# A float32 decoder trunk on one core: the preparation of its seven-product chunks in another order, and the low parts of gate slots by ScalarE's negation and a DMA that adds

## The chip, the cores and the metric

The kernel runs on one core of a Trainium2 chip. The metric is device time in microseconds. Engines are named as in the profile: PE (TensorE), DVE (VectorE), ACT (ScalarE), POOL (GpSimd) and SP (SyncE, which here issues the loads of weights). POOL also issues DMAs that add into their destination.

## What is computed

Two layers on 512 tokens of width 1024, float32. Each layer is a gated feed-forward stage, a mixing stage (sparse attention, pooling, memory attention) and a second feed-forward stage. The change lies in the four feed-forward stages:

```python
def rms_norm(x, g):
    xf = x.astype(jnp.float32)
    y = xf * lax.rsqrt(jnp.mean(xf * xf, axis=-1, keepdims=True) + EPS)
    return (y * g.astype(jnp.float32)).astype(x.dtype)

def swiglu(h, w_gate, w_up, w_down):
    return (jax.nn.silu(h @ w_gate) * (h @ w_up)) @ w_down
...
x = x + 0.5 * swiglu(rms_norm(x, ffn1_norm[l]), ffn1_gate[l], ffn1_up[l], ffn1_down[l])
```

The gate and up matrices are 1024 x 2816, the down matrix 2816 x 1024.

## The kernel before

**Arithmetic.** A float32 product is made of three PE passes on two rounded parts (`fp32r`): hi x hi, hi x lo, lo x hi (`passes`). So every operand needs a high part (ACT's rounding copy) and a low part. The low part comes in one of two ways: a subtraction value minus high on DVE or POOL; or ACT writes the rounded negative of the value into the low buffer and POOL issues a DMA that adds the value to it (`round_ahead` and `rest`).

**Tiles.** Activations are kept transposed, width on the 128 partitions, the 512 tokens along the free axis (`T`). A weight slot is 128 x 1024. SP loads slots into a ring of four in `raw`; `w_hi` and `w_lo` are rings of the same four places. 2816 is 22 chunks of 128 (`FC`); a chunk has a gate slot, an up slot and a down slot.

**A feed-forward stage.** PE first computes gate and up of 4 *classic* chunks (`CLASSIC`), slots 0 to 7, 24 matmuls of 512 columns each (`project_first`, `gate_up`). DVE takes a classic chunk out of PSUM, times the reciprocal root `r` (`evacuate`), ACT applies the silu (`classic_silu`), DVE multiplies (`gated_up`), ACT and DVE split the result for the down product (`classic_hi`, `classic_lo`). The other 18 chunks (`FAST`) are *seven-product* chunks: gate and up together are a 2 x 2 block product with seven multiplications instead of eight, halves of the width against halves of the tokens (`HALF` = 256). Each product is four 128-blocks times three passes, 12 matmuls of 256 columns.

- The token operands are `b11`, `b21`, `b22` (blocks of the normalized input `hn`, strided: four pieces of 256 columns) and `t1` to `t4` (sums of blocks, `token_sum`), all 128 x 1024, made once a stage: `op_round` on ACT for the high part, `op_rest` on DVE (`b11`, `b22`) or `rest_op` on POOL (`t1`, `b21`, `t2`, `t3`, `t4`) for the low.
- The weight operands are made for each chunk: four sums `s1` to `s4` of 128 x 512 (`weight_sum` on DVE, `sum_hi` on ACT, `rest_sum` on POOL), the gate slot itself (`gate_hi` on ACT, `gate_rest` on DVE) and the up slot's second half (`a22_hi`, `a22_rest`).
- The results are put together by `base_copy`, `silu0`, `silu1` on ACT and `up1_begin`, `up1_end`, `up0_end`, `gate1_begin`, `gate1_end`, `z_end` on DVE, half a tile each.

**Order.** Each engine runs a list written out by hand; nothing is planned at run time. PE's for period s is P1(s), P6(s), P4(s-1), P3(s-1), P2(s), P5(s), P7(s). Operands: P1 `b11`, P6 `t2`, P4 `t4`, P3 `b22`, P2 `b21`, P5 `t1`, P7 `t3`. P1 and P2 use the gate slot, P6, P5, P7 and P3 the sums 2, 1, 3 and 4. P4(0) needs `up1_begin(0)`, which needs P7(0); P2(0) needs `base_copy(0)`, which needs P1(0). Periods 0 and 1 are written out ahead of the loop, 16 follow, the last two apart on ACT and DVE. During the classic products and periods 0 and 1 the other engines make all the operands: this preparation is what the change orders anew. Then come the down products, 22 slots of 24 matmuls.

**Waits.** An engine runs its list in order, so an instruction that waits holds up all behind it. SP's refill of a gate slot waits for `s_sum_ready[4]`, DVE's last read of it. `root` makes the root of the mean square on ACT; the table for it is loaded when it gets there; DVE's reciprocal follows, and all of the preparation needs it.

Page lines: L684 is every matmul, L1643 and L1646 `evacuate`, L1653 `gated_up`, L1659 `classic_lo`, L1250 `classic_hi`, L1666 `normalize`, L1685 `token_sum`, L1691 `op_rest`, L613 `rest_op`, L1259 `op_round`, L1297 `gate_hi`, L1700 `gate_rest`, L1729 `weight_sum`, L1281 `sum_hi`, L621 `rest_sum`, L1319 `base_copy`, L1739 `up1_begin`, L1220 `root`, L549 `rest`, L1230 and L1231 `round_ahead`.

Of the kernel before, what the change touches and what calls it, by code (L numbers as in the profile page):

```python
# [128 lines left out]
def build(nc, x_t, mem_t, weights, pool_w, params, consts, out):  # L129
# [349 lines left out]
    with nc.Block() as block:  # L479

        @block.sync
        def _(sp):
# [57 lines left out]
        def _(pool):  # L540
# [66 lines left out]
            def ffn(l, e):  # L607
                base, q = FFN_BASE[e], l * 2 + e

                def rest_op(name):  # L610
# [14 lines left out]
                for n in range(BEGUN, 2 * CLASSIC):  # L625
                    rest(l, base + n)
                rest_op("t1")
                rest_op("b21")
                rest_op("t2")
                rest_sum(2, 0)  # L630
                rest_sum(1, 0)
                rest_sum(4, 0)
                rest_sum(3, 0)
                rest_op("t3")
                rest_sum(2, 1)
                rest_op("t4")
                rest_sum(1, 1)
                with pool.Fori(1, FAST - 1) as s:
# [1567 lines left out]
```

## Time and profile before

| | before |
|---|---|
| median of 3 runs | 1931.46 us (1931.42 to 1933.45) |
| profiled execution, time | 1928.9 us |
| its span | 1926.8 us |
| its mean granted clock of PE | 0.993 |
| PE busy | 1860.9 us, 97% |
| DVE busy | 1206.1 us, 63% |
| ACT busy | 1006.4 us, 52% |
| POOL busy | 744.9 us, 39% |
| `w_lo<-raw` DMAs issued by POOL | 179, of 512 KB |

Busy shares are means over stages with different limits. Where time can be won or lost is read from the stretches in which PE isn't busy, and from who was waited for there. A granted clock of 1.00 is 2.4 GHz and one of 0.50 is 1.2 GHz.

### The profile page before, as it was taken

To read this page: it belongs to the slowest core of one execution; us is meant where nothing else is said; L and a number is where in the kernel's file an instruction comes from. 1 tells how busy PE (TensorE), PEld (TensorE's weight loads), DVE (VectorE), ACT (ScalarE), POOL (GpSimd) and SP (SyncE) were. 2 spreads that over 40 slices of the span, in tenths; PEclk is the share of its full clock that TensorE was granted. 3 is DMA by queue.
4 is the path that set the end of the run, shared out by engine and by line. 5 is a ranking of instruction groups with operands and counts; after the bars stand their busy time and mean duration, and the time that the engine had idled before them with its cause. 6 is when DMAs were issued, how large, how long until landed. Compare 5 with 4: busy or idle time off the path is not lost.

```text
span 1926.8 us, 33602 instructions
## 1 busy us (share of the span) xinstructions
PE 1860.9 (97%) x11692; PEld 1633.7 (85%) x11692; DVE 1206.1 (63%) x1885; ACT 1006.4 (52%) x1610; POOL 744.9 (39%) x561
## 2 busy tenths in 40 slices
PE   7799999999999899999997999999999998999999
PEld 5799988877768699998887999888877787999887
DVE  6998821368753989841089988114786459988311
ACT  6444454575665544554464444546657564445542
POOL 2566621112511656641126666111216016666310
PEclk9899999999999999999999999999999999999999
DMA  7233388888237423368862333888781373333785
GB/s 213 79 106 103 100 202 193 184 198 193 72 88 175 120 88 109 106 161 195 193 163 77 101 100 117 206 195 196 183 203 39 86 183 110 99 109 105 181 196 140
DMA packets 75391, 272.92 MB, mean 142 GB/s; under 512 B 8496, under 2 KB 8752, under 8 KB 75056
## 3 DMA queue, kind: packets, MB, share of 16 engines
q1 hardware_dynamic: 48960, 175.67, 28.4%
q0 software_dynamic: 25776, 93.86, 27.1%
q10 hardware_dynamic: 576, 2.36, 0.3%
q8 instruction: 47, 0.77, 0.2%
q14 instruction: 32, 0.26, 0.0%
HBM read 175.91 MB, written 2.10 MB: 92 GB/s over the span
## 4 chain that ended last, share of the span: by engine, by line
PE 84%; DVE 9%; issue 3%; ACT 1%; DMA 1%; DVEq 0%; SPq 0%; ACTq 0%; POOLq 0%
PE bank L684 83%; DVE s_sum L1729 2%; PE bank L1122 1%; DVE hn L1666 1%; DMA w_lo<-raw 1%; DVE w_lo L1700 1%; DVE t L1653 1%; DVE a_hi L1659 1%; DVE t_sum L1685 1%; DVE b_lo L1691 0%; DVE h_lo L1601 0%; DVE t L1646 0%; DMA raw<-weights 0%; DVE zf L1777 0%; DVE t L1643 0%
## 5 line engine op out<-in xcount | busy, mean ns | idle before, releaser
L549 POOL DMA_DIRECT2D w_lo<-raw x179 | 154.6, 873 | 803.2 <-ACT w_lo L1231 758.1
L621 POOL TENSOR_TENSOR w_lo<-s_sum,w_hi 128x512 fp32r<-128x512 f32 x216 | 338.8, 1582 | 285.9 <-ACT w_hi L1281 285.7
L684 PE MATMUL bank<-t_hi,w_hi 128*128 128x256 f32 x1152 | 330.7, 287 | 38.3 <-DVE zf L1739 27.4
L1230 ACT ACTIVATE w_hi<-raw 128x1024 fp32r<-128x1024 f32 x163 | 172.3, 1057 | 344.3 <-PE bank L684 325.6
L684 PE MATMUL bank<-t_lo,w_hi 128*128 128x256 f32 x1152 | 328.8, 285 | 0.0
L684 PE MATMUL bank<-t_hi,w_lo 128*128 128x256 f32 x1152 | 328.7, 285 | 0.0
L684 PE MATMUL bank<-a_hi,w_hi 128*128 (+1 forms) x832 | 324.8, 390 | 0.0
L684 PE MATMUL bank<-a_lo,w_hi 128*128 (+1 forms) x832 | 323.8, 389 | 0.0
L684 PE MATMUL bank<-a_lo,w_lo 128*128 (+1 forms) x704 | 273.9, 389 | 0.0
L1281 ACT ACTIVATE w_hi<-s_sum 128x512 fp32r<-128x512 f32 x216 | 132.3, 624 | 245.4 <-DVE s_sum L1729 234.6
L684 PEld LDWEIGHTS bank<-t_hi,w_hi 128*128 128x128 f32 x1152 | 223.7, 194 | 41.8 <-issue 39.7
L1863 DVE TENSOR_TENSOR a_hi<-zf,a_lo x72 | 49.8, 692 | 327.1 <-ACT a_lo L1402 327.1
L684 PEld LDWEIGHTS bank<-t_hi,w_lo 128*128 128x128 f32 x1152 | 224.1, 194 | 0.0
L684 PEld LDWEIGHTS bank<-t_lo,w_hi 128*128 128x128 f32 x1152 | 224.0, 194 | 0.0
L684 PE MATMUL bank<-h_hi,w_hi 128*128 128x512 f32 x496 | 199.6, 402 | 13.7 <-ACT h_hi L1208 8.0
L684 PE MATMUL bank<-h_hi,w_lo 128*128 128x512 f32 x496 | 194.6, 392 | 0.0
L684 PEld LDWEIGHTS bank<-a_hi,w_hi 128*128 128x128 f32 x832 | 156.2, 188 | 33.8 <-issue 1.4
L684 PEld LDWEIGHTS bank<-a_lo,w_hi 128*128 128x128 f32 x832 | 156.2, 188 | 32.1
L684 PE MATMUL bank<-h_lo,w_hi 128*128 128x512 f32 x496 | 179.0, 390 | 0.1
L1231 ACT ACTIVATE w_lo<-raw 128x1024 fp32r<-128x1024 f32 x163 | 169.9, 1043 | 0.0
L684 PE MATMUL bank<-b_hi,w_hi 128*128 128x256 f32 x576 | 164.0, 285 | 5.0 <-ACT base_p L1319 5.0
L684 PE MATMUL bank<-b_lo,w_hi 128*128 128x256 f32 x576 | 163.6, 284 | 0.0
(206 smaller groups left out, 3958.9 us busy)
## 6 DMA issues: line engine op xcount, KB each, us to landing
raw<-weights SPq DMA_DIRECT2D x326, 512.0 KB, 3.8
w_lo<-raw POOLq DMA_DIRECT2D x179, 512.0 KB, 5.9
x<-x_t SPq DMA_DIRECT2D x4, 512.0 KB, 7.4
mem<-mem_t ACTq DMA_DIRECT2D x2, 1024.0 KB, 7.6
out_t<-x SPq DMA_DIRECT2D x8, 256.0 KB, 2.1
const<-consts SPq DMA_DIRECT2D x1, 481.5 KB, 10.5
wpool<-pool_w ACTq DMA_DIRECT2D x2, 128.0 KB, 7.5
par<-params SPq DMA_DIRECT2D x1, 38.0 KB, 3.4
```

The source lines that it names most:

```text
L549: G.dma_start(w_lo[:, s], raw[:, s], accum_op=ALU.add).then_inc(w_ready[pos], 16)
L621: G.tensor_tensor(out=fast_weight(l, e, product, 0, True), in0=s_sum[i - 1][:, :], in1=fast_weight(l, e, product, 0, False).bitcast(f32), ...
L684: return nc.tensor.matmul(out_, lhsT, rhs, start=start, stop=stop, skip_group_check=True)
L1122: last = nc.tensor.transpose(bank[2 + n % 2][:, b * P:(b + 1) * P], prob[n % 4][:, b * P:(b + 1) * P], con(C_ID, P))
L1230: nc.scalar.activation(w_hi[:, s], raw[:, s], ACT.Copy).then_inc(w_hi_done, 1)
L1231: nc.scalar.activation(w_lo[:, s], raw[:, s], ACT.Copy, scale=-1.0)\
L1281: nc.scalar.activation(fast_weight(l, e, product, 0, False), s_sum[i - 1][:, :], ACT.Copy).then_inc(s_hi_ready[i], 1)
L1653: V.tensor_tensor(out=chunk(t2, f % 2), in0=chunk(t1, f % 2), in1=chunk(t2, f % 2), op=ALU.mult).then_inc(prod_ready, 1)
L1659: V.tensor_tensor(out=chunk(a_hi, f), in0=chunk(t2, f % 2), in1=chunk(a_lo, f).bitcast(f32), op=ALU.subtract).then_inc(a_lo_ready, 1)
L1666: last = V.scalar_tensor_tensor(out=chunk(hn, k), in0=chunk(x, k), scalar=par[:, ds(l * PARAMS + (gain + k), 1)], in1=r[:, :], op0=ALU.mul ...
L1729: V.tensor_tensor(out=s_sum[i - 1][:, :], in0=a, in1=b, op=op).then_inc(s_sum_ready[i], 1)
L1863: V.tensor_tensor(out=a_hi[:, ds(f * T, T)], in0=zf[:, ds(f * T, T)], in1=a_lo[:, ds(f * T, T)].bitcast(f32), op=ALU.subtract).then_inc(a_ ...
```

## The change

- **Low parts of gate slots.** `gate_hi` also writes the negative of the slot into `w_lo`, and POOL's new `rest_gate` issues the adding DMA; DVE's `gate_rest` is gone. PE waits for the DMA, with one semaphore for even and one for odd chunks. SP's refill of a gate slot waits for it too.
- **Token operands.** `t1` and `b22` get their low part by `op_negate` (ACT) and a DMA (`rest_op`, POOL); `b21`, `t2`, `t3`, `t4` by `op_rest` on DVE. The order of `op_round`s differs, and the places of `op_hi` and `op_lo` start at `a_lo`'s beginning.
- **Low parts of sums.** Of chunk 0, and of `s2` of chunk 1, on DVE (`sum_rest`); the later ones on POOL as before.
- **Classic chunks.** `evacuate` is cut into `gate_out` and `up_out`, which stand apart. `gated_up` writes to `zf`, and the split for the down product moves to the stage's end (`split_hi`, `split_lo`). `classic_hi` and `classic_lo` are gone.
- **Root.** Its table is loaded ahead of the wait for the sums; `round_ahead(base)` stands ahead of `root` in all four stages, `round_ahead(base + 1)` ahead of the first `classic_silu`.

Cut to its core:

```diff
-        _at = (a_lo_at + (CLASSIC + 4 * _j) * tile_b) if _j < 4 else (h_at + 4 * (_j - 4) * tile_b)
+        _at = (a_lo_at + 4 * _j * tile_b) if _j < 5 else (h_at + 4 * (_j - 5) * tile_b)
...
+                    if not up:
+                        sp.wait_ge(g_lo_ready[s % 2], 16 * i + gate_lo_count(l * 2 + e, s, s % 2))
...
                 def rest_op(name):
-                    pool.wait_ge(op_hi_ready[name], q + 1)
-                    G.tensor_tensor(out=wide(op_lo[name]), in0=op_source[name],
-                                    in1=wide(op_hi[name]).bitcast(f32),
-                                    op=ALU.subtract).then_inc(op_lo_ready[name], 1)
+                    wait_apart(pool, op_neg_ready, q * len(DMA_RESTS) + DMA_RESTS.index(name) + 1)
+                    G.dma_start(wide(op_lo[name]), op_source[name], accum_op=ALU.add)\
+                        .then_inc(op_lo_ready[name], 16)
...
+                def rest_gate(s, par):
+                    wait_apart(pool, g_neg_ready, s + (q * FAST + 1))
+                    to = fast_slot(l, e, par)
+                    p = place_of(l, base + 2 * (CLASSIC + par)) * SLOT
+                    G.dma_start(w_lo[:, to:to + SLOT], raw[:, p:p + SLOT], accum_op=ALU.add)\
+                        .then_inc(g_lo_ready[par], 16)
...
-                    pe.wait_ge(g_lo_ready, at(s))
+                    pe.wait_ge(g_lo_ready[par], gate_lo_count(q, s, par))
...
             def root(l, ph):
+                nc.scalar.preload_act_table(ACT.Sqrt)
...
+                def op_negate(name):
+                    nc.scalar.activation(wide(op_lo[name]), op_source[name], ACT.Copy, scale=-1.0)\
+                        .then_inc(op_neg_ready, 1)
...
                     nc.scalar.activation(w_hi[:, to:to + SLOT], raw[:, p:p + SLOT],
                                          ACT.Copy).then_inc(g_hi_ready, 1)
+                    nc.scalar.activation(w_lo[:, to:to + SLOT], raw[:, p:p + SLOT],
+                                         ACT.Copy, scale=-1.0).then_inc(g_neg_ready, 1)
...
+                def split_hi(f):
+                    if isinstance(f, int) and f < CLASSIC:
+                        act.wait_ge(prod_ready, (q + 1) * CLASSIC)
+                        act.wait_ge(prod_done[1], at(FAST - 1))
+                    else:
+                        act.wait_ge(zf_ready, f + (q * FAST + 1 - CLASSIC))
+                    nc.scalar.activation(a_lo[:, ds(f * T, T)], zf[:, ds(f * T, T)], ACT.Copy)\
+                        .then_inc(a_hi_ready, 1)
...
+                    else:
+                        split_hi(0)
                     a22_hi(s, par)
+                    if isinstance(s, int) and s + 1 >= FAST:
+                        split_hi(1)
                     sum_hi(4, s)
...
                 silu0(FAST - 1, 1)
+                silu1(FAST - 1, 1)
+                split_hi(2)
                 round_down(3)
-                silu1(FAST - 1, 1)
+                split_hi(3)
...
+                def gate_out(f):
+                    if f >= 2:
+                        dve.wait_ge(prod_ready, q * CLASSIC + f - 1)
+                    dve.wait_ge(slot_done, l * SLOTS + base + 2 * f + (RING + 1))
...
-                    V.tensor_tensor(out=chunk(t2, f % 2), in0=chunk(t1, f % 2), in1=chunk(t2, f % 2),
+                    V.tensor_tensor(out=chunk(zf, f), in0=chunk(t1, f % 2), in1=chunk(t2, f % 2),
                                     op=ALU.mult).then_inc(prod_ready, 1)
...
                     if more:
-                        gate_rest(s + 1, 1 - par)
                         weight_sum(1, s + 1, 1 - par)
```

What this does to the lists is shown where the prediction needs it. Names there are the program's, with a buffer number behind; `base_p` is what `base_copy` writes, `s_sum1` to `s_sum4` are the sums, `bank4` and `bank0` are PSUM banks. ACT at the beginning of the seven-product chunks of the first stage, before:

```order
L1281 ACTIVATE w_hi_53<-s_sum3_69 128x512
L1259 ACTIVATE t3_hi_109<-t3_sum_99 128x1024
L1319 ACTIVATE base_p_117<-bank4 128x256
L1288 ACTIVATE w_hi_53<-raw_52 128x512
L1259 ACTIVATE b22_hi_113<-hn_96 128x1024
L1281 ACTIVATE w_hi_53<-s_sum2_68 128x512
L1259 ACTIVATE t4_hi_111<-t4_sum_100 128x1024
```

and now:

```order
L1301 ACTIVATE w_hi_53<-s_sum3_69 128x512
L1308 ACTIVATE w_hi_53<-raw_52 128x512
L1341 ACTIVATE base_p_117<-bank4 128x256
L1274 ACTIVATE t4_hi_111<-t4_sum_100 128x1024
L1301 ACTIVATE w_hi_53<-s_sum2_68 128x512
L1274 ACTIVATE b22_hi_113<-hn_96 128x1024
L1279 ACTIVATE b22_lo_114<-hn_96 128x1024
```

`t3`'s rounding and a classic `a_lo` are no longer ahead of the first `base_p`; the up slot's half is, and `b22` has two instructions, behind `t4` and `s_sum2`.

DVE at the same place, up to the first `zf` from a bank (`up1_begin(0)`), before:

```order
L1759 TENSOR_TENSOR part_u_118<-bank5,base_p_117 128x256
L1729 TENSOR_TENSOR s_sum2_68<-raw_52,s_sum1_67 128x512
L1707 TENSOR_TENSOR w_lo_54<-raw_52,w_hi_53 128x512
L1729 TENSOR_TENSOR s_sum3_69<-raw_52 128x512
L1691 TENSOR_TENSOR b22_lo_114<-hn_96,b22_hi_113 128x1024
L1729 TENSOR_TENSOR s_sum4_70<-raw_52,s_sum2_68 128x512
L1643 TENSOR_TENSOR t1_58<-bank2,r_57 128x512
L1646 TENSOR_TENSOR t2_59<-bank3,r_57 128x512
L1653 TENSOR_TENSOR t2_59<-t1_58,t2_59 128x512
L1659 TENSOR_TENSOR a_hi_55<-t2_59,a_lo_56 128x512
L1739 TENSOR_TENSOR zf_95<-bank5,base_p_117 128x256
```

and now:

```order
L1789 TENSOR_TENSOR part_u_118<-bank5,base_p_117 128x256
L1758 TENSOR_TENSOR s4_lo_116<-s_sum4_70,s4_hi_115 128x512
L1729 TENSOR_TENSOR w_lo_54<-raw_52,w_hi_53 128x512
L1758 TENSOR_TENSOR w_lo_54<-s_sum2_68,w_hi_53 128x512
L1722 TENSOR_TENSOR t4_lo_112<-t4_sum_100,t4_hi_111 128x1024
L1751 TENSOR_TENSOR s_sum3_69<-raw_52 128x512
L1677 TENSOR_TENSOR t2_59<-bank3,r_57 128x512
L1684 TENSOR_TENSOR zf_95<-t1_58,t2_59 128x512
L1751 TENSOR_TENSOR s_sum4_70<-raw_52,s_sum2_68 128x512
L1769 TENSOR_TENSOR zf_95<-bank5,base_p_117 128x256
```

The rests of `s_sum4` and `s_sum2` and of `t4` stand where sums and `b22`'s rest stood, and no `a_hi` is made here.

POOL from the last classic slots on, before:

```order
L549 DMA w_lo_54<-raw_52 128x1024 x5
L613 TENSOR_TENSOR t1_lo_108<-t1_sum_97,t1_hi_107 128x1024
L613 TENSOR_TENSOR b21_lo_106<-hn_96,b21_hi_105 128x1024
L613 TENSOR_TENSOR t2_lo_104<-t2_sum_98,t2_hi_103 128x1024
L621 TENSOR_TENSOR w_lo_54<-s_sum2_68,w_hi_53 128x512
L621 TENSOR_TENSOR w_lo_54<-s_sum1_67,w_hi_53 128x512
L621 TENSOR_TENSOR s4_lo_116<-s_sum4_70,s4_hi_115 128x512
L621 TENSOR_TENSOR w_lo_54<-s_sum3_69,w_hi_53 128x512
```

and now:

```order
L558 DMA w_lo_54<-raw_52 128x1024 x4
L622 DMA t1_lo_108<-t1_sum_97 128x1024
L558 DMA w_lo_54<-raw_52 128x1024
L638 DMA w_lo_54<-raw_52 128x1024 x2
L622 DMA b22_lo_114<-hn_96 128x4x256
L638 DMA w_lo_54<-raw_52 128x1024
L629 TENSOR_TENSOR w_lo_54<-s_sum1_67,w_hi_53 128x512
```

The seven subtractions of the first piece are gone from POOL; the second piece has DMAs for `t1`, gate slots 0 and 1, `b22` and gate slot 2.

## Rows read from the trace of the kernel before

**Rows 1.** Stretches, PE: start:end, us, busy (x instructions), PEclk, DMA share, GB/s.

```profile
59.36:94.21 34.85, 24.82 (x169) 0.85 0.20 62
654.09:687.97 33.88, 23.40 (x169) 0.90 0.21 63
1014.32:1047.89 33.57, 22.50 (x170) 0.95 0.18 63
1608.40:1641.58 33.18, 23.86 (x170) 0.90 0.22 64
94.21:252.85 158.64, 158.63 (x1320) 1.00 0.36 110
```

**Rows 2.** Timeline of PE: start, us, instruction, count, [idle before <-releaser].

```profile
35.87 0.50 PE L684 MATMUL bank<-h_hi,w_hi 128*128 128x512 f32 x1 [1.46 <-DVE t L1646]
42.90 0.50 PE L684 MATMUL bank<-h_hi,w_hi 128*128 128x512 f32 x1 [1.26 <-DMA w_lo<-raw]
...
658.56 0.39 PE L684 MATMUL bank<-b_hi,w_hi 128*128 128x256 f32 x1 [1.25 <-ACT base_p L1319]
664.10 0.35 PE L684 MATMUL bank<-t_hi,w_hi 128*128 128x256 f32 x1 [2.40 <-POOL t_lo L613]
674.34 0.55 PE L684 MATMUL bank<-t_hi,w_hi 128*128 128x256 f32 x1 [5.70 <-DVE zf L1739]
...
687.97 0.35 PE L684 MATMUL bank<-t_hi,w_hi 128*128 128x256 f32 x1 [1.14 <-DVE zf L1739]
```

**Rows 3.** Stretch after the longest wait, columns as in Rows 1.

```profile
674.30:679.30 5.00, 4.96 (x23) 0.50 0.02 3
```

**Rows 4.** Timeline of DVE in the second feed-forward stage.

```profile
623.66 3.35 DVE L1615 RECIPROCAL r<-r 128x512 f32<-128x512 f32 x1 [3.62 <-ACT r L1220]
627.16 0.69 DVE L1643 TENSOR_TENSOR t<-bank,r 128x512 f32<-128x512 f32 x1
628.37 2.73 DVE L1666 SCALAR_TENSOR_TENSOR hn<-x,par,r 128x512 f32<-128x512 f32 x4
...
642.07 3.43 DVE L1700 TENSOR_TENSOR w_lo<-raw,w_hi 128x1024 fp32r<-128x1024 f32 x1
645.42 2.89 DVE L1659 TENSOR_TENSOR a_hi<-t,a_lo 128x512 fp32r<-128x512 f32 x1
...
673.82 0.41 DVE L1739 TENSOR_TENSOR zf<-bank,base_p 128x256 f32<-128x256 f32 x1
...
688.27 1.21 DVE L1700 TENSOR_TENSOR w_lo<-raw,w_hi 128x1024 fp32r<-128x1024 f32 x1
689.40 0.68 DVE L1729 TENSOR_TENSOR s_sum<-raw 128x512 f32<-128x512 f32 x1
690.00 0.42 DVE L1759 TENSOR_TENSOR part_u<-bank,base_p 128x256 f32<-128x256 f32 x1
```

**Rows 5.** Timeline of POOL, beside the two long rows of Rows 4.

```profile
641.47 2.95 POOL L613 TENSOR_TENSOR b_lo<-hn,b_hi 128x1024 fp32r<-128x1024 f32 x1 [1.72 <-ACT b_hi L1259]
```

**Rows 6.** Timeline of ACT in the second feed-forward stage.

```profile
621.65 1.28 ACT L1220 ACT_TABLE_LOAD   x1 [4.80 <-PE bank L684]
622.94 0.69 ACT L1220 ACTIVATE r<-bank,const 128x512 f32<-128x512 f32 x1
...
630.32 1.04 ACT L1230 ACTIVATE w_hi<-raw 128x1024 fp32r<-128x1024 f32 x1
631.27 1.04 ACT L1231 ACTIVATE w_lo<-raw 128x1024 fp32r<-128x1024 f32 x1
```

**Rows 7.** Tile w_lo, POOL: landings in 600:700, in 410:600 and in 94:252.

```profile
DMA to landing us min/median/max: 4.5/6.2/8.6
...
DMA to landing us min/median/max: 4.6/6.6/11.5
...
DMA to landing us min/median/max: 4.6/4.6/4.6
```

**Rows 8.** Timeline in the loop of the second stage, ACT and PE.

```profile
774.27 1.04 ACT L1297 ACTIVATE w_hi<-raw 128x1024 fp32r<-128x1024 f32 x1
...
785.96 0.28 PE L684 MATMUL bank<-b_hi,w_hi 128*128 128x256 f32 x1
```

**Rows 9.** Timeline at the loop's end: fourth down slot's rounding, first down product.

```profile
848.96 1.06 ACT L1330 ACTIVATE w_hi<-raw 128x1024 fp32r<-128x1024 f32 x1 [0.98 <-PE bank L684]
...
850.14 0.40 PE L684 MATMUL bank<-a_lo,w_hi 128*128 128x512 f32 x1
```

More of the change, by code:

```diff
@@ L623, in rest_sum, with period @@
                                     op=ALU.subtract).then_inc(s_lo_ready[i], 1)
[L625 to L638, printed above, removed]
+                def rest_gate(s, par):
[4 more added lines that the diff above has]
+                        .then_inc(g_lo_ready[par], 16)
+                def period(s, par):
                     rest_sum(3, s)
@@ L641, in ffn @@
                     rest_sum(4, s)
+                    if not (isinstance(s, int) and s + 2 >= FAST):
+                        rest_gate(s + 2, par)
                     rest_sum(1, s + 1)
+                for n in range(BEGUN, 2 * CLASSIC - 1):
+                    rest(l, base + n)
+                rest_op("t1")
+                rest(l, base + 2 * CLASSIC - 1)
+                rest_gate(0, 0)
+                rest_gate(1, 1)
+                rest_op("b22")
+                rest_gate(2, 0)
+                rest_sum(1, 1)
+                period(1, 1)
+                with pool.Fori(1, FAST // 2 - 1) as i:
+                    period(i * 2, 0)
+                    period(i * 2 + 1, 1)
+                period(FAST - 2, 0)
                 rest_sum(3, FAST - 1)
@@ L1236, in ffn @@
                 prepare(l, 2 * e, (G_FFN1, G_FFN2)[e], base - 1)
-                ahead = l == 0 and e == 0
-                if ahead:
-                    round_ahead(l, base)
+                round_ahead(l, base)
                 root(l, 2 * e)
@@ L1778, in z_end @@
                                     op=ALU.mult).then_inc(zf_ready, 1)
[L1780 removed]
+                gate_out(0)
+                up_out(0)
                 normalize(0)
[L1782 removed]
+                gate_out(1)
                 token_sum("t1")
+                up_out(1)
+                normalize(1)
                 op_rest("b11")
[L1785 removed]
                 token_sum("t2")
                 gated_up(0)
[L1788 to L1789 removed]
+                op_rest("t2")
+                op_rest("b21")
+                token_sum("t3")
+                gate_out(2)
+                up_out(2)
                 weight_sum(1, 0, 0)
                 weight_sum(2, 0, 0)
[L1792 removed]
                 token_sum("t4")
[L1794 removed]
+                gated_up(1)
+                op_rest("t3")
                 weight_sum(3, 0, 0)
                 weight_sum(4, 0, 0)
[L1797 to L1799 removed]
+                sum_rest(2, 0)
+                sum_rest(1, 0)
+                gated_up(2)
+                gate_out(3)
+                sum_rest(3, 0)
                 weight_sum(1, 1, 1)
+                weight_sum(2, 1, 1)
                 gate1_begin(0, 0)
[L1803 removed]
+                sum_rest(4, 0)
                 a22_rest(0, 0)
+                sum_rest(2, 1)
+                op_rest("t4")
                 weight_sum(3, 1, 1)
[L1806 removed]
+                up_out(3)
+                gated_up(3)
                 weight_sum(4, 1, 1)
[L1808 to L1810 removed]
                 def period(s, par):
@@ L1838, in tail @@
                     z_end(s, par)
-                up1_begin(0, 0)
-                up1_end(0, 0)
-                gate_rest(2, 0)
-                weight_sum(1, 2, 0)
-                gate1_begin(1, 1)
-                weight_sum(2, 2, 0)
-                up0_end(0, 0)
-                weight_sum(3, 2, 0)
-                a22_rest(1, 1)
-                gate1_end(0, 0)
-                gated_up(3)
-                classic_lo(3)
-                z_end(0, 0)
-                weight_sum(4, 2, 0)
+                period(1, 1)
                 with dve.Fori(1, FAST // 2 - 1) as i:
```

97 lines of the change are left out of this document (36 added, 61 removed).

## The prediction

> **What bounds the kernel now.** I read the busy time by stretches first, since the question is where TensorE (PE) isn't full. In the loop of a feed-forward stage it is: from 94.21 it runs 1320 matmuls in 158.64 us, busy all the time at full clock [rows 1]. A product has 12 matmuls, so that is 110 products at 158.64 / 110 = 1.442 us, and a period of seven takes 10.1 us. What the change gives VectorE (DVE) there is worth nothing, unless it makes PE wait.
>
> The four stretches above it are the openings: from a stage's first product P1(0) to P4(1), the fourteenth product after it (Pn(s) is product n of chunk s). They hold 14 products, 20.19 us at the loop's pace, and take 34.85, 33.88, 33.57 and 33.18 us [rows 1]. So 14.66, 13.69, 13.38 and 12.99 us are lost, 54.7 in all. PE's timeline shows where, in the second stage: 1.25 us until ScalarE (ACT) copied `base_p`; 2.40 until POOL had `t3`'s low part; 5.70 and 1.14 until DVE wrote `zf` (`up1_begin`) [rows 2]. That is 10.5 us; the rest is the clock, which after the 5.70 us wait stands at 0.50, the lower of its levels, with 23 matmuls in 5 us [rows 3], where the loop's pace makes 42. In stage one, ahead of its opening, 1.46 us go to DVE's first emptying of banks and 1.26 to a classic slot's low part [rows 2]: 2.7 us. **What there is to gain is 54.7 + 2.7 = 57.4 us.**
>
> Why DVE is late: a 1024-wide difference takes 1.21 us when it is alone, with the next start 1.13 later, and a 512-wide sum 0.60; but 3.43 and 2.89 us (512 wide!) beside a POOL subtraction of 2.95 us [rows 4, 5]. The Trainium skill (SBUF — State Buffer, the list under its door diagram) says that a DVE instruction with two SBUF inputs and a GpSimd one that reads SBUF hold a port pair exclusively, for the whole instruction; the trace agrees: 2.89 us for one of 0.68.
>
> **The change, part by part**, in the second stage's times; t0 = 654.09 is P1(0).
>
> *DVE's queue until `up1_begin(0)`.* Before, DVE goes from 627.16 to 673.82 [rows 4], 46.7 us. Its instructions alone: 8 emptyings, 8 weight sums, 3 `gated_up`, 3 `classic_lo` and `a22_rest`, 23 at 0.60 = 13.8; 8 at 1.13 (4 token sums, 2 `op_rest`, 2 `gate_rest`) = 9.0; `normalize`, twice 2.7 [rows 4]; `gate1_begin` 0.35: 28.6 us. Most of the other 18 us is waiting beside POOL's 11 subtractions. The change takes off 2 `gate_rest`, 3 `classic_lo` and `b22`'s rest, -(2.26 + 1.8 + 1.13) = -5.2; it adds the rests of `t2`, `b21`, `t3`, `t4` and five `sum_rest`, 4.5 + 3.0 = +7.5; `gated_up(3)` comes forward, +0.6. Sum 31.5, and no POOL arithmetic stands beside it before `rest_sum(1,1)`. Starting at 627, DVE could be done at 658.6, and `up1_begin(0)` can't start before P7(0) ends at t0 + 5 x 1.442 + 0.2 = 661.5. PE wants it at P4(0), t0 + 7 x 1.442 = 664.18. Walked instruction by instruction behind what each waits for, `t4`'s rest ends at 660.5, then `weight_sum(3)`, `up_out(3)`, `gated_up(3)` and `weight_sum(4)` take 2.4, and `up1_begin` ends at 663.4: 0.8 us ahead. The waits of 5.70 and 1.14 and the slow clock go. What is late next is `b22`, below.
>
> *`t3` on DVE.* Its rest ends near 649.6, wanted at P7(0), 659.9: the 2.40 us go.
>
> *`base_copy(0)`.* ACT had `t3` in front of it; now it has `sum_hi(3,0)` and `a22_hi`, done near 655.5, when P1(0) ends (655.7). The copy is ready at 656.1 and P2(0) wants it at 657.0: the 1.25 us go. In stage one they don't: classic work starts later there, DVE reaches `gate_out(3)` 2.5 us after P1(0) starts, ACT waits for it in `classic_silu(3)`, and 0.5 + 0.5 + 0.5 + 0.3 us later comes the copy, at t0 + 4.6 where P2 wants it at t0 + 2.9. I leave **1.75 us** of wait there.
>
> *`b22` by negation and DMA, the new dependence.* ACT: P6(0) ends at 657.2; `sum_hi(2,1)` half of a 1024-wide one, 0.5, then `b22`'s rounding and negation at 0.95 each (630.32 to 631.27) [rows 6]: 659.7. POOL has only this to do, so the DMA is issued at once. P3(0) wants it at t0 + 8 x 1.442 = 665.6: it may take 5.9 us. Accumulations of the same 512 KB took 4.5 to 8.6 us around this stage, 6.2 in the middle [rows 7]. No row has one with a source in four pieces of 1 KB per partition; below nothing it can't cost, since it still has a start, a copy and an end. Bounds 4.5 and 11.5 (the longest of any stage) [rows 7]; I take 7.2, the middle row and one more for the pieces. **Wait 1.3 us** per stage, 2.1 in stage one, where ACT's lateness narrows the room to 5.1.
>
> By the Trainium skill (DMA: Bandwidth & Descriptors, the SWDGE fit) such a DMA takes about 2.0 us + bytes / 436 GB/s, 3.2 us here, and (same page, why small descriptors are slow) copies inside SBUF don't pay for short pieces. The rows' smallest, 4.5, already lies above the fit, so I don't use it; by it `b22` would cost no wait (rival 1).
>
> *`t1` and the gate slots of chunks 0 and 1.* `t1` is negated near 634 and `gate 0` near 640, both wanted after 654; gate 1 near 648.5, wanted at 661.3. Each has over 12 us for a DMA. POOL's queue puts `t1` ahead of the last classic slot's rest, 0.95 us of ACT later than before; that slot is wanted 3 us or more after it lands. Nothing.
>
> *`root`.* The table load of 1.28 us comes ahead of the wait for the sums [rows 6]. In stage one that starts DVE 1.28 earlier and takes nearly all of the 1.46 away; `round_ahead(base + 1)` now stands ahead of the first `silu`, about 3 us earlier, and takes the 1.26. In the others `round_ahead(base)`, 1.9 us, goes in front, into the 4.80 us in which ACT idled [rows 6]; 0.8 us of the load's gain are left, which no one waits for. In `mix` nobody waits for it either.
>
> *The loop.* DVE loses `gate_rest` (1.13 or more), ACT gains 0.95, POOL an issue. New is a chain: ACT's gate rounding starts at 774.27, with the negation it ends at 776.2, and the P1 that reads this slot starts at 785.96 [rows 8], so the DMA has 9.8 us; the one accumulation inside a loop took 4.6 [rows 7]. No wait. SP's refill of the slot now waits for that landing too, but the sums that it waits for anyway come at the end of DVE's period, about when P1 starts, later than this landing.
>
> *The end.* `split_hi(2)` and `silu1` go ahead of the fourth down slot's rounding, which moves from 848.96 to about 851.7 [rows 9]: in memory by 862 even at 8.6 us. Down products begin at 850.14 [rows 9] and 24 matmuls take some 5.4 us a slot, so it is wanted at 866. `split_hi(0)` and `(1)` go where ACT waited for products. Nothing.
>
> **Sum.** Stage one: 14.66 + 2.7 - 0.1 - 1.75 - 2.1 = 13.4. The others: 13.69 + 13.38 + 12.99 - 3 x 1.3 = 36.2. Gain 49.6. The profiled execution took 1928.9 us (span 1926.8), 2.6 under the median 1931.5: 1931.5 - 49.6 = **1881.9 us**.
>
> **Rivals.**
> 1. *No new wait*: `b22` lands in under 5.9 us and ACT keeps up. For it: the quickest landings, 4.5 and 4.6 us, leave over a microsecond [rows 7]. Gain 57.4 - 1.75 - 0.1 = 55.5: 1876. The fit of the Trainium skill's page DMA: Bandwidth & Descriptors would give this too.
> 2. *`b22` late*: it lands in 11.5 us. Waits 3 x 5.6 + 6.4 = 23.2; and waits of 5.7 us brought the low clock for 5 us, half of which is lost: 4 x 2.5 = 10. Gain 55.5 - 33.2 = 22.3: 1909. For it: four times as many pieces; against it: DMA share about 0.2 in the openings [rows 1].
> 3. *ACT becomes the bound of the openings*: it has three gate negations, two operand negations more by `P4(1)`, 4.8 us, and its queue stands still at every wait. If each opening keeps 3 us more of waiting, some with low clock: gain 38, 1894.
> 4. *Slower*: the loop's chain. From P2(s) to P1(s+2) the slot passes through ACT, POOL and the DMA in two periods. If landings there exceed 9.8 us, every second period waits for the excess; 4 stages x 8 pairs = 32 of them. From 9.8 + 49.6 / 32 = 11.35 us on the change is slower; with the 11.5 of rows 7 it loses 54 and ends at 1936, and each further us costs 32. For it: loads run there at a DMA share of 0.36, and an accumulation's own share comes on top. Against it: 4.6 us measured at that share.
> 5. *It doesn't do what it says*: the openings are bound by something the walk misses, and half of the gain comes: 1906.
>
> **How the numbers follow.** Forecast 0.55, rival one 0.15, two 0.08, three 0.12, four 0.04, five 0.06. Leaving out the slow end of two and five, and four, the range is 1874 to 1903. About 0.2% (3.9 us) is what a measurement of this kernel can tell from no change. Faster 0.94, same 0.02, slower 0.04.
>
> **What would show it.** Right: the openings (P1(0) to P4(1)) take 22 to 24 us, with no `zf` wait and full clock; one wait on a DMA of `b_lo` remains at P3(0); the loop still runs 1320 matmuls in 158.6 us; DVE idles before `up1_begin(0)`; 512-wide DVE instructions of the opening take 0.7 us. Wrong: loop products wait for the DMA of `w_lo`; PE waits for ACT's `base_p` or `w_hi` in every stage; landings of the strided copy above 9 us.

## The result, and the profile after

The changed kernel takes 1918.57 us (median of 4 runs, 1917.35 to 1918.94), the kernel before, measured again beside it, 1932.26 (1931.42 to 1933.45): a ratio of 0.9928, 95% interval 0.991 to 0.9945. It is faster by 13.7 us, where the prediction had 49.6, and above the range. The profiled execution took 1918.83 us, its span 1916.9.

The openings gave what was forecast in sum, and the loops didn't stay as they were. First the stretches, as in [rows 1] (start:end, us, busy of PE, PEld, DVE, ACT and POOL with their instructions, PEclk, DMA share, GB/s; PEld is PE's loading of weights). Two openings, each with the loop behind it, then the loops of stages three and four:

```profile
56.80:80.89 24.09, 22.11 (x169) 21.73 (x168) 18.95 (x30) 15.20 (x25) 9.51 (x8) 0.93 0.72 164
80.89:248.73 167.84, 161.44 (x1322) 159.02 (x1320) 117.59 (x172) 86.51 (x156) 100.97 (x78) 1.00 0.57 145
651.17:671.82 20.65, 20.38 (x169) 20.20 (x168) 16.29 (x25) 14.40 (x24) 9.34 (x8) 1.00 0.67 161
671.82:839.60 167.78, 161.17 (x1322) 158.92 (x1320) 117.33 (x172) 86.26 (x156) 101.17 (x78) 1.00 0.57 145
...
1030.50:1198.30 167.80, 161.15 (x1322) 158.91 (x1320) 117.56 (x172) 86.47 (x156) 100.40 (x77) 1.00 0.56 144
1622.10:1789.90 167.80, 161.31 (x1322) 158.98 (x1320) 117.53 (x172) 86.48 (x156) 100.99 (x78) 1.00 0.58 145
```

The openings of stages one and two fell from 34.85 and 33.88 us to 24.09 and 20.65, at a granted clock of 0.93 and 1.00; those of stages three and four went from 33.57 and 33.18 to 22.71 (1007.79 to 1030.50) and 20.75 (1601.35 to 1622.10). That is 47.3 us, and stage one's P1(0) starts at 56.80 instead of 59.36, 2.6 more. But each loop, 158.64 us before, takes 167.8: 9.2 us more in each of the four, 36.7 in all. 47.3 + 2.6 - 36.7 = 13.2.

PE's waits (what it waited for, us in total, times, longest) have one entry for the loops. Of its 29.3 us some 26 lie in them; the other part of the 36.7 stands in PE's busy time, 161.2 to 161.4 us a loop where it was 158.6:

```profile
PE bank L705 <- DVE zf L1769: 29.3, 51, 1.1
```

The waits of the openings, where [rows 2] had 1.25, 2.40, 5.70 and 1.14 us in one stage, are these four and a fifth, of 0.36 us, in stage four:

```profile
61.57 0.38 PE L705 MATMUL bank<-b_hi,w_hi 128*128 128x256 f32 x1 [1.73 <-ACT base_p L1341]
...
72.19 0.36 PE L705 MATMUL bank<-b_hi,s_hi 128*128 128x256 f32 x1 [0.24 <-DMA b_lo<-hn]
...
663.11 0.36 PE L705 MATMUL bank<-b_hi,s_hi 128*128 128x256 f32 x1 [0.27 <-DMA b_lo<-hn]
...
1020.34 0.35 PE L705 MATMUL bank<-t_hi,w_hi 128*128 128x256 f32 x1 [2.31 <-issue]
```

Why is the loop longer? Nothing in it waits for a landing; PE waits for DVE's `zf` (`up1_begin`) once a period. So I followed DVE back, through one period of stage one's loop. ACT, POOL and DVE (timelines: start, us, line, ..., idle before and its releaser):

```profile
120.01 1.05 ACT L1317 ACTIVATE w_hi<-raw 128x1024 fp32r<-128x1024 f32 x1
120.95 1.04 ACT L1319 ACTIVATE w_lo<-raw 128x1024 fp32r<-128x1024 f32 x1
121.90 1.14 ACT L1301 ACTIVATE w_hi<-s_sum 128x512 fp32r<-128x512 f32 x2
...
130.51 0.42 ACT L1334 ACTIVATE gated<-gated 128x256 f32<-128x256 f32 x1 [1.30 <-DVE gated L1796]
130.83 1.04 ACT L1317 ACTIVATE w_hi<-raw 128x1024 fp32r<-128x1024 f32 x1
...
122.57 0.87 POOL L638 DMA_DIRECT2D w_lo<-raw  x1 [2.10 <-ACT w_lo L1319]
123.18 2.83 POOL L629 TENSOR_TENSOR w_lo<-s_sum,w_hi 128x512 fp32r<-128x512 f32 x2
...
124.91 1.66 DVE L1751 TENSOR_TENSOR s_sum<-raw 128x512 f32<-128x512 f32 x1 [2.42 <-POOL w_lo L629]
126.49 0.41 DVE L1789 TENSOR_TENSOR part_u<-bank,base_p 128x256 f32<-128x256 f32 x1
...
128.72 1.42 DVE L1729 TENSOR_TENSOR w_lo<-raw,w_hi 128x512 fp32r<-128x512 f32 x1 [0.29 <-ACT w_hi L1308]
130.06 0.41 DVE L1796 TENSOR_TENSOR gated<-bank,part_u 128x256 f32<-128x256 f32 x1
```

Read as a ring: ACT rounds a gate slot (120.01) and negates it (120.95 to 121.99). POOL starts the DMA on it 0.58 us later, 122.57. Behind that in POOL's queue stands subtraction 1, 123.18, and DVE's sum 1 of the next chunk waits for it, since it overwrites the sum that the subtraction reads: DVE is idle for 2.42 us. Sum 1 starts at 124.91; behind it in DVE's queue are sums 2 and 3, `a22_rest` and `gate1_end`, ending near 130.5; ACT's `silu1` waits for `gate1_end`, and behind `silu1` stands the next gate rounding, 130.83. The ring is 10.82 us round; PE's work in it is 10.10.

Before, the first half was two instructions shorter. ACT went from the gate rounding at 774.27 straight to `sum_hi(1)`, and POOL straight to the subtraction:

```profile
775.22 0.61 ACT L1281 ACTIVATE w_hi<-s_sum 128x512 fp32r<-128x512 f32 x1
...
775.91 3.54 POOL L621 TENSOR_TENSOR w_lo<-s_sum,w_hi 128x512 fp32r<-128x512 f32 x2 [1.18 <-ACT w_hi L1281]
...
777.07 1.22 DVE L1700 TENSOR_TENSOR w_lo<-raw,w_hi 128x1024 fp32r<-128x1024 f32 x1
778.21 1.78 DVE L1729 TENSOR_TENSOR s_sum<-raw 128x512 f32<-128x512 f32 x1
```

From the gate rounding to the start of subtraction 1 it was 1.64 us, now 3.17; from there to sum 1 the way got shorter, so that the gate rounding to sum 1 took 3.94 us and takes 4.90. The instruction that the change takes off DVE, `gate_rest` at 777.07, stood in between: subtraction 1 was done at 777.21, and sum 1 came 1.0 us later, behind `gate_rest`.

### The profile page after: what moved, and what is told of

Same layout as the page of the kernel before. It is cut to its first block and busy times, and to the rows that moved or that the text cites. A ratio compares the mean times of both kernels' runs of the same rounds, so it can differ in the third digit from the quotient of the medians.

```text
span 1916.9 us, 33816 instructions
## 1 busy us (share of the span) xinstructions
PE 1863.9 (97%) x11692; PEld 1630.5 (85%) x11692; DVE 1074.6 (56%) x1845; ACT 1069.5 (56%) x1690; POOL 672.8 (35%) x601
## 5 line engine op out<-in xcount | busy, mean ns | idle before, releaser
L705 PE MATMUL bank<-t_hi,w_hi 128*128 128x256 f32 x1152 | 330.6, 287 | 31.9 <-DVE zf L1769 29.3
L629 POOL TENSOR_TENSOR w_lo<-s_sum,w_hi 128x512 fp32r<-128x512 f32 x200 | 277.8, 1494 | 153.1 <-ACT w_hi L1301 153.0
L1301 ACT ACTIVATE w_hi<-s_sum 128x512 fp32r<-128x512 f32 x216 | 127.3, 621 | 257.9 <-DVE s_sum L1751 256.9
L1690 DVE TENSOR_TENSOR a_hi<-zf,a_lo (+1 forms) x88 | 68.4, 781 | 321.9 <-ACT a_lo L1363 321.8
L1751 DVE TENSOR_TENSOR s_sum<-raw 128x512 f32<-128x512 f32 x144 | 160.4, 1114 | 146.4 <-POOL w_lo L629 146.4
```

The costliest lines, as they stand in the source:

```text
L629: G.tensor_tensor(out=fast_weight(l, e, product, 0, True), in0=s_sum[i - 1][:, :], in1=fast_weight(l, e, product, 0, False).bitcast(f32), ...
L705: return nc.tensor.matmul(out_, lhsT, rhs, start=start, stop=stop, skip_group_check=True)
L1301: nc.scalar.activation(fast_weight(l, e, product, 0, False), s_sum[i - 1][:, :], ACT.Copy).then_inc(s_hi_ready[i], 1)
L1690: V.tensor_tensor(out=a_hi[:, ds(f * T, T)], in0=zf[:, ds(f * T, T)], in1=a_lo[:, ds(f * T, T)].bitcast(f32), op=ALU.subtract).then_inc(a_ ...
L1751: V.tensor_tensor(out=s_sum[i - 1][:, :], in0=a, in1=b, op=op).then_inc(s_sum_ready[i], 1)
```

## The experiments

**Theory (ring).** The loop's period is the longer of PE's 10.10 us and this ring, and what was added to it is ACT's negation and POOL's DMA issue ahead of subtraction 1. **Rivals.** The negation alone sets it; the added traffic of the DMAs slows the engines or the loads; or the new order of the preparation does it, whatever is done with the gates.

**Both behind subtraction 1** (e1). ACT negates behind `sum_hi(1)`, POOL issues the DMA behind `rest_sum(1)`:

```diff
 # ACT
-                    gate_hi(s + 2, par)            # with the negation in it
+                    gate_hi(s + 2, par)
 ...                 sum_hi(1, s + 1)
+                    gate_neg(s + 2, par)
 # POOL, period
+                    rest_sum(1, s + 1)
                     if not (isinstance(s, int) and s + 2 >= FAST):
                         rest_gate(s + 2, par)
-                    rest_sum(1, s + 1)
```

> Edit to the changed kernel: in each period ACT's negation of the gate slot stands behind its rounding of sum 1, and POOL's adding DMA behind its subtraction for sum 1. Theory C (a ring of waits around the engines): in the changed kernel's loop each period takes 10.83 us, the length of a ring ACT gate rounding 0.95, negation 0.95, rounding of sum 1, POOL's DMA issue 0.61, its subtraction for sum 1, DVE's sum 1 of the next chunk and what follows on DVE, ACT's silu, gate rounding. Without the negation and the issue it is 9.27, under PE's 10.10, so the loop goes back to 10.10 a period and 158.6 us a stage instead of 167.8: 1918.6 - 37 = 1882 us. Rival D (the added DMA traffic slows the loop: DMA share 0.57 instead of 0.36): nothing moved but the order, 1915 to 1920. Rival O (the new openings hand the loop over in a worse phase): as D.

1881.87 us (1880.06 to 1883.72), ratio 0.9751 (0.9734 to 0.9767). The whole loss is gone, with the same DMAs and the same instructions. PE's waits for `zf` are 2.4 us in 4 times, one near each loop's end.

**One half each** (e2, e6). In e2 only POOL's half of that edit, ACT's as in the changed kernel; in e6 only ACT's half.

> Edit to the changed kernel: POOL's part alone, the adding DMA behind the subtraction for sum 1; ACT's list as in the changed kernel. Theory C: the ring shrinks by 0.61 us (DMA issue to the next start on POOL), to 10.22, 0.12 over PE's 10.10; of 37 us some 31 come back: about 1888 us. If ACT's negation alone made the loss, nothing: 1918. Rival D or O: 1915 to 1920.

> Edit to the changed kernel: ACT's part alone, the negation behind the rounding of sum 1; POOL still issues the DMA ahead of its subtraction for sum 1. Theory R: POOL's list is in order and the DMA now waits 0.52 us longer for the negation, so the ring grows to about 11.35 us a period: 14 periods x 4 x 0.52 = 29 more, 1948 us. If ACT's delay of the rounding of sum 1 were the cause by itself: 1882.

e2: 1914.69 us (1914.48 to 1915.14), ratio 0.9921 (0.9904 to 0.9937); I had expected 1888, and was wrong. By its time alone the rival that the negation by itself makes the loss would stand; e7 below takes it away. e6: 1950.34 us (two runs, 1949.47 and 1951.2), ratio 1.0098 (1.0078 to 1.0118), as expected: gate roundings at 110.68 and 122.04, so the period is 11.36. There the negation, one `sum_hi` later, still has subtraction 1 queued behind it through the DMA issue.

Why e2 gained nearly nothing stands in its timelines, POOL's, then DVE's:

```profile
120.60 1.29 POOL L629 TENSOR_TENSOR w_lo<-s_sum,w_hi 128x512 fp32r<-128x512 f32 x1 [2.12 <-ACT w_hi L1301]
121.83 0.87 POOL L638 DMA_DIRECT2D w_lo<-raw  x1
122.44 1.59 POOL L629 TENSOR_TENSOR w_lo<-s_sum,w_hi 128x512 fp32r<-128x512 f32 x1
...
122.03 2.56 DVE L1751 TENSOR_TENSOR s_sum<-raw 128x512 f32<-128x512 f32 x1 [1.53 <-POOL w_lo L629]
```

DVE's sum 1 is released earlier, but it begins 0.20 us after POOL's DMA issue, with subtraction 3 right behind the issue, and takes 2.56 us instead of the 1.66 of the changed kernel: it ends 0.56 us behind subtraction 3 (124.03). What was won ahead of sum 1 is lost in it.

In e1 POOL's order is the same, and sum 1 takes 2.56 us in some periods there too, and 0.68 in others. POOL, then DVE:

```profile
109.34 0.87 POOL L638 DMA_DIRECT2D w_lo<-raw  x1
...
119.49 0.87 POOL L638 DMA_DIRECT2D w_lo<-raw  x1
...
109.53 2.56 DVE L1761 TENSOR_TENSOR s_sum<-raw 128x512 f32<-128x512 f32 x1
...
119.63 0.68 DVE L1761 TENSOR_TENSOR s_sum<-raw 128x512 f32<-128x512 f32 x1
```

But without the negation ahead it starts 3.28 us after the gate rounding (106.25), where it is 4.02 in e2, and that leaves room for the long sum: the next gate rounding comes at 116.40, 10.15 us on, the one after it 10.01 us later.

**One more copy on ACT** (e3). In ACT's list, behind the gate's rounding and negation, one more 1024-wide copy, to a tile that no one reads:

```diff
+                        nc.scalar.activation(spare[:, :], raw[:, ...], ACT.Copy)
```

> Edit to the changed kernel: one more ACT copy of 128x1024 (0.95 us) into unused memory, between the gate rounding and the negation in each period. Theory C: every period becomes 10.83 + 0.95 = 11.78 us, and the periods wait from the loop's start: some 15 periods x 4 stages x 0.95 = 57 us more: 1975 us. Rival D or O, where ACT with 4 us of idle time a period is no link: no change, 1915 to 1922.

1923.49 us (1921.91 to 1927.72), ratio 0.9968 (0.9951 to 0.9986): 4.9 us above the changed kernel, not 56. The expectation speaks of a copy between rounding and negation, where it would delay the DMA; built was a copy behind both, which delays `sum_hi(1)` alone. So the run does not test the 57 us, but it says which leg of the ring is the long one:

```profile
121.84 1.04 ACT L1414 ACTIVATE spare<-raw 128x1024 fp32r<-128x1024 f32 x1
122.79 1.14 ACT L1302 ACTIVATE w_hi<-s_sum 128x512 fp32r<-128x512 f32 x2
...
122.51 0.87 POOL L639 DMA_DIRECT2D w_lo<-raw  x1 [2.10 <-ACT w_lo L1320]
123.50 2.54 POOL L630 TENSOR_TENSOR w_lo<-s_sum,w_hi 128x512 fp32r<-128x512 f32 x2
```

The copy delays `sum_hi(1)` by 0.9 us, but POOL spends most of that time on the DMA anyway (0.58 us to start it, 0.6 until the next instruction starts). Subtraction 1 starts 0.99 us after the issue instead of 0.61, and sum 1 1.42 us after that (124.92) instead of 1.73; the period is 10.91 instead of 10.82. ACT's way to subtraction 1 runs beside POOL's and had slack for most of the copy. The long leg is negation, start of the DMA, its issue.

**POOL's half, done otherwise** (e7). So the DMA must go out of the way of subtraction 1, and of sum 1 too: behind subtractions 1 and 3. ACT's list is that of the changed kernel.

```diff
 # POOL, period
                     rest_sum(3, s)
+                    if not (isinstance(s, int) and s == 1):
+                        rest_gate(s + 1, 1 - par)
                     rest_sum(2, s + 1)
                     rest_sum(4, s)
-                    if not (isinstance(s, int) and s + 2 >= FAST):
-                        rest_gate(s + 2, par)
                     rest_sum(1, s + 1)
```

> Edit to the changed kernel: POOL issues a gate slot's DMA behind both subtractions (sums 1 and 3); ACT's list as in the changed kernel, with the negation ahead of sum 1. Theory R: sum 1's subtraction starts when its rounding is done, 0.9 us sooner, nothing of POOL's DMA stands between it and DVE's next sum 1, as it did with the DMA between the two subtractions (there DVE's instruction took 2.56 us): ring 9.9 us, under PE's 10.10: 1882 us. If the negation's 0.95 us on ACT is enough for the loss: 1910 to 1918.

1882.08 us (1881.49 to 1882.51), ratio 0.9745 (0.9729 to 0.9762): as good as e1, with the negation where it was. POOL, then DVE:

```profile
118.91 2.55 POOL L629 TENSOR_TENSOR w_lo<-s_sum,w_hi 128x512 fp32r<-128x512 f32 x2 [2.12 <-ACT w_hi L1301]
121.40 0.86 POOL L638 DMA_DIRECT2D w_lo<-raw  x1
...
120.35 1.66 DVE L1751 TENSOR_TENSOR s_sum<-raw 128x512 f32<-128x512 f32 x1 [0.87 <-POOL w_lo L629]
```

The gate rounding stands at 116.32 in this trace, so it is 4.03 us to sum 1 instead of 4.90. By that I estimate the ring at 10.82 - 0.87 = 9.95 us, below PE's 10.10; the loop shows only PE's period, so its own length can't be read there. The place of one DMA issue in POOL's queue is worth 36.5 us.

**Smaller DMAs** (e4, one run). Order and count as in the changed kernel, but in the gate slots of the seven-product chunks the DMA covers 64 of the 1024 columns; the rest stays the negated value, so this computes something else.

```diff
-                    G.dma_start(w_lo[:, to:to + SLOT], raw[:, p:p + SLOT], accum_op=ALU.add)\
+                    G.dma_start(w_lo[:, to:to + 64], raw[:, p:p + 64], accum_op=ALU.add)\
```

> Edit to the changed kernel: the adding DMA of a gate slot covers 64 of its 1024 columns (the rest of the low part isn't made, so the output is not the reference's); same instructions, same waits. Theory R (ring through ACT's negation and POOL's DMA issue, 0.58 us to its start and 0.87 for it, ahead of the subtraction for sum 1): bytes are no link of it, period stays 10.8 us, time 1912 to 1920. Rival D (traffic of the added DMAs slows the loop): period 10.10, about 1882.

1917.91 us, against 1918.57: taking 15/16 of these DMAs' bytes away gives nothing back that one run could show, where the rival wanted 36 us. And e1 and e7 lose nothing with all of the bytes.

**The gates of the loop on DVE** (e5). The preparation of the changed kernel, its gates 0 and 1 by DMA, and from gate 2 on the kernel before's `gate_rest` on DVE:

```diff
 # ACT: gate_hi rounds only; gate_neg(0, 0) and gate_neg(1, 1) stand in the opening
 # POOL, period
-                    if not (isinstance(s, int) and s + 2 >= FAST):
-                        rest_gate(s + 2, par)
 # DVE, period
+                        gate_rest(s + 1, 1 - par)
```

> Edit to the changed kernel: its preparation stays, with gate slots 0 and 1 by negation and DMA, but from chunk 2 on DVE subtracts the gate slot's low part as in the kernel before. Theory C: no negation and no issue in the ring; the loop takes 158.6 us a stage and the openings keep what they gained: 1882 us. Rival O (the openings spoil the loop): loops stay over 160 us and the time stays above 1900.

1884.47 us (1881.75 to 1884.92), ratio 0.9761 (0.9745 to 0.9777). So the gain of the change is the preparation's, and the gate slots of the loop bring no more to it than the 2.4 us between this run and e7 (1882.08), whose ranges overlap. From the gate rounding to sum 1 it is 4.02 us here, with `gate_rest` in between, as in e7 without it.

**The gates alone** (e8). The kernel before with its own preparation, and all gate slots by negation and DMA, issued ahead of subtraction 1:

```diff
 # in the kernel before; ACT
+                    nc.scalar.activation(w_lo[:, to:to + SLOT], raw[:, p:p + SLOT],
+                                         ACT.Copy, scale=-1.0).then_inc(g_neg_ready, 1)
 # POOL, period
+                    if not (isinstance(s, int) and s + 2 >= FAST):
+                        rest_gate(s + 2, par)
                     rest_sum(1, s + 1)
 # DVE, period
-                        gate_rest(s + 1, 1 - par)
```

> The kernel before, with its own preparation, and the change's second half alone: the low part of every gate slot of the seven-product chunks by ScalarE's negation and GpSimd's accumulating DMA, issued ahead of subtraction 1 as in the changed kernel. The ring theory says that the loop's period becomes 10.8 us here too, whatever prepares it: 9.2 us more in each of four loops, 37 in all, while the openings shed at most a few us with three 1024-wide VectorE differences less: 1950 to 1968 us, 1958 the likeliest. The rival, that the new preparation leaves the loop in another phase and the gate slots alone would be harmless, says 1925 to 1932 us.

1966.06 us (1965.49 to 1967.68), ratio 1.0187 (1.0169 to 1.0204): 35.1 us slower than the kernel before. ACT's gate roundings at 779.24 and 790.08 and POOL's DMA issues at 770.96 and 781.80 give the period: 10.84. Four times 9.2 is 36.8, so about 2 us came back elsewhere, presumably in the openings; they weren't measured apart. The loss is the same without the new preparation.

**Better openings, two tries** (e9, e10). e9 is e1 with two edits in the opening: ACT's `classic_silu(3)`, which waits for DVE, behind `base_copy(0,0)`, and gate 2's negation and DMA behind `sum_hi(1,1)` and subtraction 1. e10 is e7 with the first of the two alone.

```diff
 # ACT, opening; both
-                classic_silu(3)
                 sum_hi(3, 0, 2 * CLASSIC - 1)
                 a22_hi(0, 0)
                 base_copy(0, 0)
+                classic_silu(3)
 # POOL, opening; e9
+                rest_sum(1, 1)
                 rest_gate(2, 0)
-                rest_sum(1, 1)
```

> The kernel with both late (1881.87 us) with two more edits: the last classic silu behind the first base_copy on ACT (takes the 1.7 us wait of the first opening), and gate slot 2's negation and DMA behind sum 1 as in the loop (may take the 2.3 us wait of the third opening). Expected 1878 to 1881 us.

> The version with GpSimd's DMA behind subtractions 1 and 3, and in the opening one edit of the combined version alone: classic_silu(3) behind base_copy(0,0). ScalarE's queue in stage one's opening then comes two microseconds earlier, and so does GpSimd's first subtraction. If the combined version lost its gain because GpSimd's work now stands beside VectorE's normalization and weight sum 4 (a wait of 3.56 us at P4(0) of stage one in place of 0.52), that wait comes here too, base_copy's 1.3 goes, and the time is 1882 to 1885 us. If it lost it by its other edit in the opening (the gate's DMA behind subtraction 1 there), the wait stays at 0.5 and the time is 1879 to 1881 us.

e9: 1884.28 us (1883.05 to 1885.09), ratio 0.9754 (0.9738 to 0.977), no better than e1. e10: 1876.47 us (1874.8 to 1877.23), ratio 0.9723 (0.9706 to 0.9739), the fastest here. Both lose `base_copy`'s wait in stage one (1.3 us in e1 and e7). In e9 a wait of 3.56 us at P4(0) of stage one takes its place; in e10 it is 1.19. DVE in e9, then in e10, the same two instructions (`zf<-t,t` of the emptying and weight sum 4):

```profile
65.79 1.82 DVE L1693 TENSOR_TENSOR zf<-t,t 128x512 f32<-128x512 f32 x1
67.54 2.23 DVE L1760 TENSOR_TENSOR s_sum<-raw,s_sum 128x512 f32<-128x512 f32 x1
```

```profile
64.78 0.69 DVE L1684 TENSOR_TENSOR zf<-t,t 128x512 f32<-128x512 f32 x1
65.39 0.68 DVE L1751 TENSOR_TENSOR s_sum<-raw,s_sum 128x512 f32<-128x512 f32 x1
```

In e9 subtraction 1 comes first (65.39 to 67.05), and DVE's two instructions stand beside it, the DMA issue and the next subtraction. In e10 POOL issues the DMA at 65.33 and subtracts from 65.89 on, and DVE is just ahead. So e9's other edit did the harm in this place, as the second reading in e10's expectation had it; the wait did not stay at 0.5 though, and the time is lower still than that reading gave. Of the 5.6 us from e7 to e10 the traces show 1.3 less for `base_copy`, 0.7 more at P4(0), and stage three's wait of 2.31 us gone: 2.9; the waits for `b22` take 0.3 of it back. The rest of it I haven't placed. (In the profiled executions stage one's P1(0) also starts at 55.09 in e10 and at 57.14 in e7, but e2's shows such an early start too, without e10's edit, so I don't count it.)

## Why the prediction was wrong, step by step

- **The openings: right in sum, in part by luck.** Forecast were 49.6 us; measured are 47.3 + 2.6 = 49.9. That it comes so close is luck: the errors of the terms below, 5.1 us one way and 1.7 + 2.3 the other, nearly cancel. They last 20.65 to 24.09 us, forecast 22 to 24; the clock is at 1.00 in three of them and 0.93 in stage one. The waits for `zf` of 5.70 and 1.14 us are gone, but one comes back in stage three (below). DVE's 512-wide instructions take 0.68 and 0.69 us there, all but one. With the loop mended (e1, e7) the time is 1881.9 and 1882.1 us, which is the number predicted for the change.
- **`base_copy` in stage one**: forecast 1.75, measured 1.73. In the other stages none, as said. What I left out is the clock behind it, though [rows 3] had shown it behind a longer wait:

```profile
62.00:66.00 4.00, 4.00 (x24) 4.00 (x23) 3.44 (x7) 3.13 (x5) 0.00 (x0) 0.62 0.02 7
```

  24 matmuls in 4 us, where the loop's pace makes 33, at a clock of 0.62, most of it at the lower level. From P2(0) at 61.57 to P3(0) at 72.19 are six products, 8.65 us; less the wait of 0.24 they took 10.38, so 1.7 us go there. In e7, behind a wait of 1.31 us, the same stretch has 35 matmuls at 1.00.
- **`b22`**: the size was off. The DMA from four pieces landed in 5.6 us (median of four, the longest 6.1), where I had taken 7.2; the waits are 0.24 to 0.36 in three stages and none in stage three, instead of 1.3 (2.1 in stage one). Rival one, 5.9 us or less, was right on this. That gives back 6.0 - 0.9 = 5.1 us.
- **`issue` in stage three**, 2.31 us at P4(0): not forecast. It is a late `zf` all the same: DVE's weight sum 4 took 3.82 us there, `up1_begin(0)` behind it ran from 1019.82 to 1020.23, and P4(0) started at 1020.34:

```profile
1016.08 3.82 DVE L1751 TENSOR_TENSOR s_sum<-raw,s_sum 128x512 f32<-128x512 f32 x1
...
1015.92 0.88 POOL L638 DMA_DIRECT2D w_lo<-raw  x1 [0.43 <-issue]
1016.48 2.85 POOL L629 TENSOR_TENSOR w_lo<-s_sum,w_hi 128x512 fp32r<-128x512 f32 x2
```

- **The loop: this step failed.** "New is a chain ... so the DMA has 9.8 us ... No wait." The chain from the negation to the product that reads the slot is right, and no product waited for it. But I gave "ACT gains 0.95, POOL an issue" no price, since I measured them against PE's reader alone. What stands behind them in the two queues is `sum_hi(1)` and subtraction 1, which DVE's sum 1 needs, and from there a ring leads back to the same gate rounding. With the issue out of its way (e7) I estimate that ring at 9.95 us, 0.15 under PE's 10.10; with the issue in it, it is 10.82, 0.72 us a period above PE's, and 51 periods with a wait make 36.7 us. How much the ring before had to spare no row shows; ACT and DVE wait for PE's banks in it (776.14 after 0.31 us, 776.20 after 0.32), so it was not what set the pace. Three questions would have shown it (what is queued behind the moved instruction, on each engine; who waits for that; does that lead back): I asked them for the openings and not for the loop.
- **"DVE loses `gate_rest` (1.13 or more)"** was no gain, and I priced none. The 1.1 us that it frees go into waiting for POOL, 2.42 us a period in the changed kernel and 0.87 in e7; e5, which has `gate_rest` back, is no slower by more than 2.4 us in all.
- **Rival four** named the right place and the wrong mechanism: there are no landings above 9.8 us. In the loop they take 5.5 us at the median, at a DMA share of 0.56 to 0.58 instead of 0.36. Its sign did not come either, since 36.7 us of loss stay below the openings' 49.9.
- **The chances.** Faster, at 0.94, is what came. The range ended at 1903, because I put every doubt into the openings; the doubt of the loop, 36.7 us wide, stood at 0.04 and was left out.
- Of the difference in span, 9.9 us, the stretches account for 13.2. Of the 3.3 us between, 1.2 lie between the first loop's end and stage two's first product (402.44 us, before 401.24), and as much between the third and stage four's (403.05, before 401.87): the down products, the mixing stage and the next classic products. I haven't traced them.

## What to carry to other kernels

When work is moved from an engine in a loop to two others, don't ask only whether its result is in time: write down what stands behind it in each in-order queue, who waits for that, and follow that on until it either ends or comes back to the same instruction one period later. Such a ring has a length of its own, and a loop whose busiest engine shows no idle time says nothing about how close the ring is; one DMA issue of 0.87 us, ahead of two subtractions instead of behind them, was worth 36.5 us of 1918. And an instruction taken off an engine that doesn't set the period gives nothing by itself: DVE went from `gate_rest` to waiting.

## What the runs showed of the hardware

- **POOL's subtraction can hold up a DVE instruction that started ahead of it, when a DMA issue stands before the subtraction.** A DVE instruction of 0.68 us with two inputs in SBUF took 2.56 us (e2) and 3.82 us (stage three of the changed kernel) when it started 0.20 and 0.16 us after POOL began to issue a DMA, with a subtraction 0.61 and 0.56 us behind the issue's start. Both ended 0.56 to 0.57 us after POOL's last subtraction. In stage four of the changed kernel the same weight sum 4 also started 0.16 us after the issue (1609.47 and 1609.63), but the subtraction came 0.95 us behind the issue, and it took 0.68. And an issue with no subtraction behind it held up nothing (the kernel before, then the changed one, POOL and DVE):

```profile
40.24 0.86 POOL L549 DMA_DIRECT2D w_lo<-raw  x1 [1.03 <-ACT w_lo L1231]
40.71 1.21 DVE L1691 TENSOR_TENSOR b_lo<-hn,b_hi 128x1024 fp32r<-128x1024 f32 x1
...
1002.90 0.86 POOL L638 DMA_DIRECT2D w_lo<-raw  x1 [7.74 <-ACT w_lo L1319]
1003.63 0.69 DVE L1751 TENSOR_TENSOR s_sum<-raw 128x512 f32<-128x512 f32 x1
```

  1.21 and 0.69 us are what these two take alone. So it is the subtraction that holds DVE, not the issue. Where the subtraction stands close behind, the start matters too: in e7's stage one DVE's instruction started 0.07 us after the issue and took 0.69, in stage three of e10 it started 0.09 before and took 0.68, and in e1 0.14 after gave 0.68 and 0.19 after 2.56. Other rows of e1 fall on either side between 0.12 and 0.22 us, so no bound can be read. The Trainium skill (SBUF — State Buffer, the list under its door diagram) says that whoever starts first holds the shared pair of ports for the whole instruction. The ends agree with that, since DVE finishes 0.56 us behind the subtraction; the order of the starts does not, since by the profile DVE started 0.40 us ahead of it (1016.08 and 1016.48). Why, no run here shows.
- **Start of a DMA from POOL.** Where POOL was idle and waited for ACT's negation, the issue started 0.58 us after the negation's end (121.99 to 122.57), which is time in a chain that the instruction's own 0.87 doesn't show.
- **A source in four pieces.** The issue of `b22`'s DMA takes 1.30 us instead of 0.87, and it lands in 5.6 us at the median, beside the 5.4 to 5.5 of gate slots in one piece.
